# Diffusion-transformer layer on one core: the last two modulation blocks are summed between the top-value search and the routing

## The reference

```python
mod = silu(c) @ w_ada + b_ada                  # 2048 x 12288, one vector
sh1, sc1, g1, sh2, sc2, g2 = split(mod, 6)
x  = x + g1 * attention(modulate(rms_norm(x), sh1, sc1))
h2 = modulate(rms_norm(x), sh2, sc2)
s1, i1 = top_k(scores of half 1, 16);  s2, i2 = top_k(scores of half 2, 16)
cand = s1[:, None] + s2[None, :];      top_s, pos = top_k(cand, 16)
g = softmax(top_s)                             # 8 heads x 16 experts a token
y = sum over chosen e of g[e] * gelu(h2 . u[e]) * v[e]      # 16384 experts
out = rms_norm(x + g2 * y)
```

## Time and profile before

| | us |
|---|---|
| median of 3 runs (lowest, highest) | 2293.31 (2292.7, 2295.07) |
| the profiled execution: its own time | 2292.91 |
| its span, first to last instruction | 2291.1 |
| around the span | 1.8 |
| TensorE busy in the span | 2211.5 (97%) |
| VectorE busy | 1587.5 (69%) |
| ScalarE busy | 1211.5 (53%) |
| GpSimd busy | 100.2 (4%) |
| mean granted TensorE clock | 0.987 of full speed |

### The profile page before, as it was taken

One profiled execution on the slowest core, in us unless ns is written; L12 is line 12 of the kernel. 1 busy time (PEld: TensorE's weight loads), 2 busy tenths in 40 slices (PEclk: granted clock), 3 DMA queues, 4 the chain that ended last, 5 costly groups with the idle time before them and its releaser, 6 DMA issues.

```text
span 2291.1 us, 43555 instructions
## 1 busy us (share of the span) xinstructions
PE 2211.5 (97%) x14034; PEld 1952.9 (85%) x14034; DVE 1587.5 (69%) x2903; ACT 1211.5 (53%) x2131; POOL 100.2 (4%) x87
## 2 busy tenths in 40 slices
PE   4899999899999999999999999999999999999997
PEld 0478887668989999999999999998888888888886
DVE  5377767786674688788578788785666666555554
ACT  3232234575454677777665565655555555555553
POOL 0000000000000000000211111110000000000000
PEclk8899999899999999999999999999999999999998
DMA  9878876202755455555544444445766766555652
GB/s 387 338 268 282 281 251 235 99 1 76 275 200 183 150 176 187 183 182 183 169 157 162 156 156 162 157 157 210 248 238 238 242 243 238 193 193 193 193 193 81
DMA packets 123891, 453.26 MB, mean 198 GB/s; under 512 B 14400, under 2 KB 15168, under 8 KB 123200
## 3 DMA queue, kind: packets, MB, share of 16 engines
q1 hardware_dynamic: 123840, 452.63, 58.1%
HBM read 448.38 MB, written 4.19 MB: 198 GB/s over the span
## 4 chain that ended last, share of the span: by engine, by line
PE 92%; DVE 4%; DMA 2%; issue 1%; ACT 0%; SPq 0%; DVEq 0%
PE PS L668 84%; PE PS L925 3%; DMA ada_t<-w_ada 1%; PE PS L824 1%; DVE st L1209 1%; PE PS L798 1%; PE PS L675 1%; PE PS L711 1%; PE PS L651 1%; DMA raw<-stream 1%; PE PS L812 1%; PE PS L912 0%; DVE ot L1544 0%; DVE oT_l L1322 0%; DVE O L1254 0%
## 5 line engine op out<-in xcount | busy, mean ns | idle before, releaser
L367 ACT ACTIVATE w_hi<-raw 128x512 fp32r<-128x512 f32 x1296 | 816.7, 631 | 901.8 <-PE PS L668 891.0
L1008 DVE TENSOR_TENSOR w_lo<-raw,w_hi 128x512 fp32r<-128x512 f32 x1296 | 884.5, 691 | 557.8 <-ACT w_hi L367 542.1
L668 PE MATMUL PS<-h_h,w_hi 128*128 128x256 f32 (+1 forms) x2304 | 657.8, 285 | 2.1 <-DVE h_l L1038 2.1
L668 PE MATMUL PS<-h_h,w_lo 128*128 128x256 f32 (+1 forms) x2304 | 651.8, 283 | 0.0
L668 PE MATMUL PS<-h_l,w_hi 128*128 128x256 f32 (+1 forms) x2304 | 651.7, 283 | 0.0
L668 PEld LDWEIGHTS PS<-h_h,w_hi 128*128 128x128 f32 x2304 | 441.9, 192 | 3.1 <-issue 2.6
L668 PEld LDWEIGHTS PS<-h_l,w_hi 128*128 128x128 f32 x2304 | 442.1, 192 | 0.0
L668 PEld LDWEIGHTS PS<-h_h,w_lo 128*128 128x128 f32 x2304 | 441.8, 192 | 0.0
L668 PE MATMUL PS<-w_hi,p_hi 128*128 128x512 f32 x1024 | 398.5, 389 | 0.0
L668 PE MATMUL PS<-w_hi,p_lo 128*128 128x512 f32 x1024 | 398.3, 389 | 0.0
L668 PE MATMUL PS<-w_lo,p_hi 128*128 128x512 f32 x1024 | 398.3, 389 | 0.0
(11 more groups left out here) (198 smaller groups left out, 2250.6 us busy)
## 6 DMA issues: line engine op xcount, KB each, us to landing
raw<-stream SPq DMA_DIRECT2D x648, 512.0 KB, 3.4
ada<-w_ada SPq DMA_DIRECT2D x96, 512.0 KB, 4.5
ada_t<-w_ada SPq DMA_DIRECT2D x64, 512.0 KB, 9.4
ada_v<-w_ada SPq DMA_DIRECT2D x32, 512.0 KB, 4.3
x_c<-x_ctx SPq DMA_DIRECT2D x1, 2048.0 KB, 7.7
x<-x_lat SPq DMA_DIRECT2D x1, 2048.0 KB, 15.1
x_scratch<-x SPq DMA_DIRECT2D x1, 2048.0 KB, 7.3
x<-x_scratch SPq DMA_DIRECT2D x1, 2048.0 KB, 8.6
```

The costliest lines, as they stand in the source:

```text
L367: nc.scalar.activation(w_hi[:, (2 * j + hf) % SPLIT, :], raw[:, j, hf * HALF:(hf + 1) * HALF], ACT.Copy).then_inc(S["w_high"], 1)
L668: ins = mm(out_, l_, r_, start=(start and q == 0), stop=(stop and q == 2), skip_group_check=check)
L1008: V_.tensor_tensor(w_lo[:, h % SPLIT, :], raw[:, h // 2 % RAW, at_:at_ + HALF], w_hi[:, h % SPLIT, :].bitcast(F32), ALU.subtract).then_inc ...
```

## The change

Blocks 6 and 7 move from V to U, into turns 24 to 31. `GATES_AT` falls from 29 to 23: each step of the search is followed by three half units instead of four or five. `ROUTE_AT` stays 32 (23 + 1 + 8). Each of the eight turns holds four operations of the sum, one ahead of every two half units, and four extra loads. Their buffers `ada_u` (R + 112 KB) and `acc_u` (R + 88 KB) lie on tiles of `A` that must be 1.0 by turn 32, so POOL's eight memsets now wait for the column sums (`ada_col` of 8). The 16 column sums stand on PE between turn 31 and the transposes of the gates. V and the tail lose all of it.

The buffers:

```diff
-        ada_v = at("ada_v", [P, 2, UNIT], F32, R + 128 * KB)
-        acc_v = at("acc_v", [P, 2, UNIT], F32, R + 160 * KB)
+        ada_u = at("ada_u", [P, ADA, UNIT], F32, R + 112 * KB)
+        acc_u = at("acc_u", [P, 2, UNIT], F32, R + 88 * KB)
```

On SyncE:

```diff
+            with sp.Fori(U_Q // 4 + 1, 34 + LATE_ADA_AT) as b:
                 units(b)
             sp.wait_ge(S["x2_out"], 16)
+            for r in range(8):
+                units(34 + LATE_ADA_AT + r)
+                for q in range(ADA):
+                    n = LATE_ADA + 4 * r + q
+                    if r:
+                        sp.wait_ge(S["ada2_used"], n - 3)
+                    sp.dma_start(ada_u[:, q, :], w_ada_flat[64 + n]).then_inc(ada_in[q], 16)
+            with sp.Fori(42 + LATE_ADA_AT, U_V // 4 + 4) as b:
+                units(b)
...
-                    sp.wait_ge(S["ada2_used"], 2 * r + (LATE_ADA + s - 1))
-                    sp.dma_start(ada_v[:, s, :], w_ada_flat[2 * r + (64 + LATE_ADA + s)]).then_inc(ada_in[s], 16)
```

On GpSimd:

```diff
             pool.wait_ge(S["top_s_ready"], 1)
-            pool.wait_ge(S["x2_out"], 16)
+            nc.gpsimd.memset(acc_u[:], 0.0).then_inc(S["ada_zeroed"], 2)
+            pool.wait_ge(S["ada_col"], 8)
             for i in range(2 * ROUTE_AT, NE_TILES, 8):
                 nc.gpsimd.memset(A[:, i:i + 8, :], 1.0).then_inc(S["tiles_one"], 1)
```

On TensorE, after turn 31:

```diff
             first_product(0, ROUTE_AT, False)
+            ada_columns(6, 6, acc_u)
+            ada_columns(7, 7, acc_u)
```

On TensorE, in the tail:

```diff
-            pe.wait_ge(S["y_kept_a"], 1)
-            ada_columns(6, 3, acc_v)
-            ada_columns(7, 3, acc_v, 8)
             for c in range(4):
-                pe.wait_ge(S["y_kept_a"], min(c + 2, 4))
+                pe.wait_ge(S["y_kept_a"], c + 1)
                 pe.wait_ge(S["y_kept_d"], c + 1)
```

On VectorE, in the search (two of the four places):

```diff
                     top16(tops[:, t, h, :], pos[:, h, :], cand[:, h, :], cand2[:])
-                    next_low(5)
+                    next_low(3)
...
-                    next_low(4)
+                    next_low(3)
```

On VectorE, behind the gates:

```diff
+            def late_add(c, kt, q):
+                dve.wait_ge(ada_in[q], 4 * kt + 16 * (4 * c + 1))
+                dve.wait_ge(S["ada2_used"], kt + (16 * c + q))
+                V_.scalar_tensor_tensor(acc_u[:, c % 2, :], ada_u[:, q, :], modc[:, bass.ds(kt + q, 1)],
+                                        acc_u[:, c % 2, :], ALU.mult, ALU.add).then_inc(S["ada2_used"], 1)
+            dve.wait_ge(S["ada_zeroed"], 8)
+            for c in (6, 7):
+                b0 = 34 + LATE_ADA_AT + 4 * (c - 6)
+                with dve.Fori(0, 4) as r:
+                    for q in range(4):
+                        late_add(c, 4 * r, q)
+                        split_low(r + (b0 + q // 2), (q + 2) % 4)
+                dve.wait_ge(S["ada2_used"], 16 * c + 16)
+                dve.sem_inc(S["ada_sum"], 1)
+            ada_keep(6, 6)
+            ada_keep(7, 7)
             dve.wait_ge(S["gates_turned"], 1)
```

The turns:

```diff
-GATES_AT = 29
-ROUTE_AT = 32
+GATES_AT = 23
+LATE_ADA_AT = GATES_AT + 1
+ROUTE_AT = LATE_ADA_AT + 8
```

More of the change, by code:

```diff
@@ L308, in _ @@
             sp.dma_start(x2_dram, x[:]).then_inc(S["x2_out"], 16)
-            with sp.Fori(U_Q // 4 + 1, U_V // 4 + 4) as b:
+            with sp.Fori(U_Q // 4 + 1, 34 + LATE_ADA_AT) as b:
                 units(b)
             sp.wait_ge(S["x2_out"], 16)
+            for r in range(8):
[7 more added lines that the diff above has]
+                units(b)
             sp.wait_ge(S["w_free"], 2 * U_V + SPLIT)
             sp.dma_start(x2[:], x2_dram).then_inc(S["x2_in"], 16)
[L314 to L317, removed]
-                    sp.wait_ge(S["ada2_used"], 2 * r + (LATE_ADA + s - 1))
-                    sp.dma_start(ada_v[:, s, :], w_ada_flat[2 * r + (64 + LATE_ADA + s)]).then_inc(ada_in[s], 16)
-            with sp.Fori(U_V // 4 + 4 + 2 * KT, U_END // 4) as b:
+            with sp.Fori(U_V // 4 + 4, U_END // 4) as b:
                 units(b)
@@ L356, in _ @@
                 distance(4 * g)
-            pool.wait_ge(S["route_used"], T // 4)
-            pool.wait_ge(S["gelu_in"], NE_TILES - 2 * ROUTE_AT + 2)
-            nc.gpsimd.memset(acc_v[:], 0.0).then_inc(S["ada_zeroed"], 2)
         @block.scalar
@@ L631, in _ @@
             act.wait_ge(S["v_done"], 1)
-            for c in (3, 0, 1, 2):
+            for c in range(4):
                 nc.scalar.activation(y_tok[:, 0, c * HALF:(c + 1) * HALF], PS[:, c, :], ACT.Copy).then_inc(S["y_kept_a"], 1)
@@ L960, in experts_in @@
                     pe.wait_ge(S["routed"], T // 4 + 2)
+                if k == 6:
+                    pe.wait_ge(S["ada_col_kept"], 8)
             open_banks(experts_in)
@@ L974, in _ @@
             close_banks().then_inc(S["v_done"], 1)
-            pe.wait_ge(S["y_kept_a"], 1)
-            ada_columns(6, 3, acc_v)
-            ada_columns(7, 3, acc_v, 8)
             for c in range(4):
-                pe.wait_ge(S["y_kept_a"], min(c + 2, 4))
+                pe.wait_ge(S["y_kept_a"], c + 1)
                 pe.wait_ge(S["y_kept_d"], c + 1)
-                if c == 3:
-                    pe.wait_ge(S["ada_col_kept"], 8)
                 for k in range(4 * c, 4 * c + 4):
@@ L1425, in _ @@
             dve.sem_inc(S["gates_ready"], 1)
-            next_low(2 * (U_U + 2 + 4 * (GATES_AT + 1)) - half[0])
-            low_turns(34 + GATES_AT + 1, ROUTE_AT - GATES_AT - 1)
+            next_low(2 * (U_U + 2 + 4 * LATE_ADA_AT) - half[0])
+            def late_add(c, kt, q):
[14 more added lines that the diff above has]
+            ada_keep(7, 7)
             dve.wait_ge(S["gates_turned"], 1)
@@ L1487, in _, with value_turn @@
             p_low(1, 1)
[L1490 to L1519, removed]
+            def value_turn(b):
+                split_low(b + 98, 2)
+                split_low(b + 98, 3)
+                p_low(2 * b + 2, 0)
+                split_low(b + 99, 0)
+                split_low(b + 99, 1)
+                p_low(2 * b + 3, 1)
+            with dve.Fori(0, N_V // 4 - 1) as b:
+                value_turn(b)
             split_low(161, 2)
@@ L1530, in _ @@
             keep_rows(0)
-            dve.wait_ge(S["ada_col"], 8)
-            V_.tensor_tensor(mod[:, 5 * KT:6 * KT], PS[:, 3, 0:KT], b_ada[:, 5 * KT:6 * KT], ALU.add
-                             ).then_inc(S["ada_col_kept"], 2)
             keep_rows(1)
-            dve.wait_ge(S["ada_col_kept"], 8)
             for k in range(KT):
```

## The result

| | before | after |
| --- | --- | --- |
| median of the runs, us | 2293.34 (2292.7 to 2295.07) | 2309.64 (2309.49 to 2310.06) |
| the profiled execution: own time | 2292.91 | 2309.67 |
| its span | 2291.1 | 2307.9 |
| from the start of the first long piece of U to the start of V | 800.12 | 821.31 |
| V | 696.56 | 696.60 |

The changed kernel takes 1.0070 times as long (95% interval 1.0053 to 1.0088), 16.3 us more. The forecast was 2310.5.

The account below looks back on a forecast made before the run. The prediction took TensorE, busy for 97% of the span, to bound the kernel. Its terms, -5.0 + 0 + 4.9 + 0 + 15.3 + 2.35 = +17.6 on 2292.91, gave 2310.5 us, with a range from 2303 to 2319.

Parts of the forecast that it names:

- Tail, -5.0: In the tail, transposes and combination start earlier without the 16 column sums: -5.0 us, between 2.6 and 5.2 saved.
- what would show it: Signs expected in the profile after, among them the tail's combination 1.9 us behind V's end and not 6.9.
- V, 0: In V, removing 32 VectorE operations and 32 loads gains 0, since TensorE waits for nothing there.
- Search, +4.9: In U's search, candidate steps outlast three half units and early slack can't be kept: +4.9 us, between 0 and 8.
- Turns 24 to 31, 0: In U's eight turns with the moved sums, VectorE's operations and the loads at 363 GB/s fit: 0 us.
- The rival of the loads: In turns 24 to 31 the loads bind: at 335 GB/s eight turns take 8 us more, 2318; chance 0.12.
- Seam, +15.3: Between turn 31 and the first routing, column sums, memsets and `hotB` run in a chain, 21.5 against 6.27: +15.3 us.
- clock, +2.35: Behind the seam's idle stretch of some 12 us, TensorE's matmuls run with the clock at 0.50: +2.35 us.
- The upper bound of this part: At the seam, clock included: 20 us, with 5.2 for the column sums and twice the clock loss.
- The search is free: In U's search, VectorE holds its lead through the candidates and 4.9 falls away: 2305.6 us; chance 0.15.
- The memsets are short: At the seam, memsets run several times faster beside an idle VectorE: 2294 with them near 0; chance 0.04.
- The seam is longer: At the seam, column sums run at half clock and the clock stays low longer: up to 2315 us; chance 0.09.

Follow-up runs that it names:

- tail_alone: The kernel before without the tail's 16 column sums and their part of the last gate, `y_tok` copied in the change's order: 2289.38 us, 0.9981.
- search_alone: The kernel before with only the denser search of the change (three half units behind each step, `GATES_AT` 23): 2298.79 us, 1.0024.
- paced: The changed kernel with the search's half units dealt by step length, more behind candidates and fewer behind keys: 2309.99 us, 1.0062.
- warm: The changed kernel with 44 matmuls of zeros on TensorE while it would stand idle before the routing: 2309.86 us, 1.0073.
- early5: The changed kernel with five of the eight memsets of `A` ahead of the wait for the column sums, three behind it: 2303.44 us, 1.0043.
- turn_earlier: The changed kernel with early5 and paced together, and search and sums one turn earlier (`GATES_AT` 22): 2296.69 us, 1.0009.
- sums_apart: turn_earlier with block 6's column sums three turns ahead of block 7's, and each sum signalled one half unit earlier: 2294.87 us, 1.0004.
- loads10: The changed kernel with two more unused 512 KB loads in each of turns 24 to 31, ten instead of eight: 2321.96 us, one run.

## Why the prediction was right, point by point

- **Tail, -5.0.** The trace has -5.7, tail_alone's medians -5.0. Counted from the end of V, the transposes came 4.8 us earlier and the combination 5.4, about as said: the first transposes ran at full clock now, and the combination followed them by 0.67 us and not 1.21. But the column sums' 5.17 us held a loss of clock themselves; they took 3.75 in search_alone, whose tail is only 4.35 us longer than the changed kernel's. So the size of this term depends on the execution that it is read from. I had feared that the fall of the clock would now meet the last products, up to 2.4 us, and in the changed kernel it did not fall there at all; in tail_alone it did, and cost 1.2 there. The 6.9 and 1.9 us of "what would show it" count from the end of the eight matmuls that close V (2259.57); by that count the combination came at 1.5.
- **V, 0.** 696.60 for 696.56.
- **Search, +4.9.** 4.5 in the changed kernel, 4.5 alone. The mechanism, slack that comes first and can't be kept, is what paced bears out: with nearly the same half units in another distribution all but 0.7 us of the stalls go. The waits stand in two groups, one for each half of the tokens, as forecast, with 2.2 and 2.3 us where I took 2.4 (twice that is 4.8, and the sum's 4.9 a slip of rounding).
- **Turns 24 to 31, 0.** 0.1202 us for a matmul, no loss, at 365 GB/s. The rival of the loads was priced as bandwidth, and the queue's limit was indeed 410. What I had not seen is how thin the time between issue and use had become: VectorE waited for blocks in the changed kernel itself, for 0.3 to 7.8 us by execution, and for 7.3 to 12.3 in the three kernels with a cleaner search and the same order of loads. TensorE lost 1.1 us by it at most.
- **Seam, +15.3, and clock, +2.35.** Together 17.65; measured 16.7 to the start of V. The column sums took 3.49 where I took 4.0, the memsets 13.99 where I took 14.04, from `hotB` to the next product it was 4.25 where I took 3.44, since that piece ran at half clock, and 0.9 came behind. So the clock cost 1.8 here (warm), where I took 2.35, the loss of twelve other matmuls near the start. The upper bound of this part was added up wrongly: 5.2 for the sums and twice the clock's loss give 21 and not 20.
- **The rivals.** "The search is free" fell by search_alone. "The memsets are short" fell: 13.99 us with VectorE idle, 14.04 with VectorE at work; early5 shows that each of them, 1.74 us, is on the path. "The seam is longer" fell with the 3.49 us of column sums.

The sum of the terms of U to V and the tail was +17.6 and the trace has +15.6. The terms of the search, the seam and the tail were each taken 0.4 to 1.0 us too high. Of the 16.8 between the two profiled executions, 1.2 lies ahead of U, with a dip of the clock behind attention that no term stood for. So the hit within 0.9 us is in part luck. The mechanism of each term is borne out by the traces, and the sizes too, with the reservation on the tail above.

## What to carry to other kernels

Work that moves into another stage's buffers takes the resets of those buffers along: here taking the work out of V and the tail was worth 5 to 6 us, all of it in the tail, and a GpSimd memset of ones, which no line of the sums' own code mentions, stood behind it and in front of the routing for 14 us. Ask of every buffer that is lent out what must be written into it before its owner comes back, on which queue that stands, and who waits; split it, and do early what isn't lent. Mean load says little for a search in which the cheap steps come first, since a lead can be no longer than the buffers between the engines, here four half units. And at nearly 90% of the queue's rate it is worth looking at the order of the loads: their sum fitted, and VectorE still waited for single blocks.

## What the runs showed of the hardware that was not expected

- Column sums, matmuls with one column each, count as busy time in the profile, but the clock did not hold through 16 of them: turn 31 behind them took 13.63 us for 11.54 (turn_earlier), and 11.63 behind eight (sums_apart). At the seam the clock fell behind the 16 as well, to 0.50 from about 1140 us, while TensorE had not paused, and so it did in early5 and warm. That is another fall than the one within the pause of 11.5 us: between the two the clock was back at 1.00, and only the second went away when the pause was filled (warm).
- Shortening that pause did not shorten the work at low clock. With 11.5 us idle the 48 matmuls behind the first routing took 6.61 us, with 2.9 us idle right ahead of it (early5) 7.61. The clock was low from about 1150.0 to 1160.2 us in the first and from 1148.1 to 1155.0 in the second, which is shorter, but hardly any of it was idle time.
- One queue held 409 to 411 GB/s for most of eight turns (loads10). Below that rate, at 365 GB/s, the time from issue to landing of 512 KB had a median of 5.8 to 6.7 us over the executions of the changed kernel and of `warm`, 7.0 in paced, and 5.4 with the order changed.
- GpSimd's memset of 128x2048 takes the same time beside an idle VectorE. The Trainium skill says as much for work of these kinds (SBUF — State Buffer, "Who interferes with whom"), and here the trace agrees, with 13.99 against 14.04 us for eight.
